# A two-layer decoder step on one core: the first query half split into prompt and sample columns, and two memory key blocks transposed, inside the norm ahead of the attention

## What is computed

```
x = post_norm(x, mixer(x), ln_g[l, 0], ln_b[l, 0])
c = memory_cross_attention(x, mem_ks[l], mem_vs[l], w_q[l], w_o[l])

def post_norm(x, h, g, b):          # per token over 1024 features
    z = DN_ALPHA * x + h
    z = (z - mean(z)) * rsqrt(var(z) + LN_EPS)
    return z * g + b

def memory_cross_attention(x, mem_k, mem_v, w_q, w_o):
    q = (x @ w_q).reshape(B, T, 4, 256)
    s = einsum('bthd,bmhd->bhtm', q, mem_k) * 256 ** -0.5
    p = softmax(s)
    o = einsum('bhtm,bmhd->bthd', p, mem_v).reshape(B, T, 1024)
    return o @ w_o
```

## Time and profile before

| | |
|---|---|
| median of 3 runs | 1392.79 us (1392.18 to 1393.89) |
| the profiled execution, its own time | 1392.58 us |
| its span, first to last instruction | 1390.8 us |
| matmul engine busy | 1341.8 us (96%) |
| vector engine busy | 1019.4 us (73%) |
| scalar engine busy | 756.2 us (54%) |
| granted matmul clock, mean | 0.996 |

### The profile page before, as it was taken

One profiled execution on the slowest core, in us unless ns is written; L12 is line 12 of the kernel. 1 busy time (PEld: TensorE's weight loads), 2 busy tenths in 40 slices (PEclk: granted clock), 3 DMA queues, 4 the chain that ended last, 5 costly groups with the idle time before them and its releaser, 6 DMA issues.

```text
span 1390.8 us, 19714 instructions
## 1 busy us (share of the span) xinstructions
PE 1341.8 (96%) x7671; PEld 1114.8 (80%) x7671; DVE 1019.4 (73%) x1100; ACT 756.2 (54%) x775; POOL 149.5 (11%) x211
## 2 busy tenths in 40 slices
PE   8999999999898999999999999999899999999996
PEld 6798997788676888888887798779777788888884
DVE  4546757763578988898887356782658989898986
ACT  4444623423425876767676353332534777677765
POOL 5200246210000000000000014220000000000000
PEclk9999999999999999999999999999999999999998
DMA  9784454437964999999994455444983799999981
GB/s 284 246 269 151 150 170 138 134 124 262 371 232 155 362 360 338 352 349 348 342 359 141 134 188 178 133 161 175 372 320 131 283 368 336 356 343 342 358 319 38
DMA packets 102002, 353.67 MB, mean 254 GB/s; under 512 B 6368, under 2 KB 32496, under 8 KB 72224
## 3 DMA queue, kind: packets, MB, share of 16 engines
q1 hardware_dynamic: 97056, 336.09, 67.4%
q0 software_dynamic: 4864, 16.45, 3.5%
HBM read 332.85 MB, written 19.67 MB: 253 GB/s over the span
## 4 chain that ended last, share of the span: by engine, by line
PE 81%; DVE 8%; ACT 4%; DMA 3%; POOL 2%; issue 2%; SPq 0%; DVEq 0%; ACTq 0%; POOLq 0%
PE ps L1895 65%; DMA att_kt<-in_cache_mem_v 2%; PE ps L2263 1%; PE ps L2473 1%; PE ps L2286 1%; DVE mix_s L1604 1%; PE ps L2274 1%; PE ps L1904 1%; PE ps L1903 1%; PE ps L2005 1%; DVE x L1324 1%; DVE x L1321 1%; PE ps L2095 1%; PE ps L2416 1%; PE ps L2417 1%
## 5 line engine op out<-in xcount | busy, mean ns | idle before, releaser
L1895 PE MATMUL ps<-w_hi,xt_hi 128*128 128x512 f32 x576 | 229.6, 399 | 5.9 <-DVE w_lo L1261 2.2
L1257 DVE TENSOR_TENSOR w_lo<-raw,w_hi 128x2048 fp32r<-128x2048 f32 x62 | 141.5, 2294 | 125.4 <-ACT w_hi L837 125.4
L1895 PE MATMUL ps<-w_hi,xt_lo 128*128 128x512 f32 x576 | 225.5, 391 | 0.0
L1895 PE MATMUL ps<-w_lo,xt_hi 128*128 128x512 f32 x512 | 200.4, 391 | 0.0
L837 ACT ACTIVATE w_hi<-raw 128x2048 fp32r<-128x2048 f32 x64 | 121.7, 1913 | 143.7 <-PE ps L1895 58.0
L1261 DVE TENSOR_TENSOR moe_lo<-moe_in_raw,w_hi 128x2048 fp32r<-128x2048 f32 x72 | 164.2, 2290 | 22.6 <-ACT w_hi L844 22.6
L1261 DVE TENSOR_TENSOR w_lo<-raw,w_hi 128x2048 fp32r<-128x2048 f32 x72 | 164.8, 2291 | 16.6 <-ACT w_hi L844 16.2
L844 ACT ACTIVATE w_hi<-moe_in_raw 128x2048 fp32r<-128x2048 f32 x72 | 138.1, 1918 | 56.4 <-PE ps L1895 56.4
L844 ACT ACTIVATE w_hi<-raw 128x2048 fp32r<-128x2048 f32 x72 | 137.5, 1912 | 14.8 <-PE ps L1895 14.8
L1895 PE MATMUL ps<-xt_hi,w_hi 128*128 128x320 f32 x448 | 138.6, 309 | 0.2
L1895 PE MATMUL ps<-xt_hi,w_lo 128*128 128x320 f32 x448 | 138.4, 309 | 0.0
(11 more groups left out here) (408 smaller groups left out, 2574.0 us busy)
## 6 DMA issues: line engine op xcount, KB each, us to landing
raw<-in_moe_w_gate SPq DMA_DIRECT2D x48, 1024.0 KB, 5.0
moe_in_raw<-in_moe_w_down SPq DMA_DIRECT2D x48, 1024.0 KB, 4.9
moe_in_raw<-in_moe_w_up SPq DMA_DIRECT2D x32, 1024.0 KB, 5.6
raw<-in_moe_w_up SPq DMA_DIRECT2D x32, 1024.0 KB, 5.6
raw<-in_hgrn_w_in SPq DMA_DIRECT2D x16, 1024.0 KB, 5.5
raw<-in_cache_mem_k SPq DMA_DIRECT2D x16, 1024.0 KB, 6.0
moe_in_raw<-in_moe_w_gate SPq DMA_DIRECT2D x16, 1024.0 KB, 5.8
raw<-in_moe_w_down SPq DMA_DIRECT2D x16, 1024.0 KB, 4.9
```

The lines of the kernel that those rows point to most:

```text
L1257: nc.vector.tensor_tensor(lo_at(slot_of(k)), raw_at(slot_of(k)), hi_at(hi_slot(k)).bitcast(F32), ALU.subtract).then_inc(w_low, 1)
L1895: ins = mm(out, lhs, rhs, start=start and n == 0, stop=stop and n == 2, skip_group_check=shared)
```

## The change

- SP loads key blocks 0 and 1 (`EARLY = 2`) into the probability tile `att_p`, once the memset has marked it as free, behind the first query chunk and ahead of the second. The later stream of loads has seven key blocks.
- The matmul engine transposes the eight quarters of these blocks inside `block_norm`: two behind tile 0's transposes, three behind tile 1's, three more behind a first part of the queries. The fillers of this norm go (those of the other norm stay).
- The first query half is cut in three: rows 0 to 255 for the 256 prompt columns behind tile 1's transposes, rows 256 to 511 for the prompt columns behind tile 2's, and all four groups of rows for the 64 sample columns once tile 2 is split.
- The vector engine splits tile 1 between the sample tile's addition and its statistics, in place of behind its norm.
- The scalar engine makes all eight copies of the early quarters, and the high part of the second query chunk, inside the norm.
- POOL makes the low part of the second query chunk too.
- The attention begins with key block 2, then the prompt's scores, then blocks 3 to 5.

```
+EARLY = 2
+KEYS = BATCHES - EARLY
+KV_CHUNKS = KEYS + 2
+EARLY_BANKS = (4, 7, 5, 4, 7, 5, 4, 6)
...
         # SP
-                dense(done, last, groups)
+                dense(done, done + 1, groups)
+                sp.wait_ge(at_z, l + 1)
+                for n in range(EARLY):
+                    sp.dma_start(early_keys(n).rearrange("p (t u c) -> p t u c", t=2, u=2), memory(l, "k", n)).then_inc(first_in[n], 16)
+                dense(done + 1, last, groups)
...
         # POOL
-                split_query(chunk_no(first_block(l) + IN_BLOCKS[l] + 2), groups)
+                for half in range(2):
+                    split_query(chunk_no(first_block(l) + IN_BLOCKS[l] + 2) + half, groups)
...
         # ACT, layer_norm; q % 3 == 0 is the norm behind the mixer
+                def keys_early(pieces):
+                    for i in pieces:
+                        n, s = i // 4, i % 4
+                        act.wait_ge(at_tr, 4 * BATCHES * (q // 3) + i + 1)
+                        nc.scalar.activation(st_att["kt"][:, n, 2 * s:2 * s + 2, :], ps[:, EARLY_BANKS[i], :].rearrange("p (b m) -> p b m", b=2),
+                                             ACT.Copy).then_inc(at_kv if s % 2 else at_ka, 1)
...
+                if q % 3 == 0:
+                    keys_early(range(0, 2))
...
+                if q % 3 == 0:
+                    turned(u, 1)
+                    split(splits[0], groups)
+                    splits[0] += 1
+                    keys_early(range(2, 3))
                 tile_rstd(q, 2)
+                if q % 3 == 0:
+                    keys_early(range(3, 8))
...
         # DVE, block_norm, between tile 2's addition and its statistics
                         ins.then_inc(evac[par], 1)
+                        if q % 3 == 0:
+                            turned(u, 1)
...
         # PE
+            def query_products(db, groups, kts, first, last):
+                k = chunk_no(db)
+                pe.wait_ge(w_low, at(k + 1, groups, GCH))
+                for kt in kts:
+                    for n in range(4):
+                        cols = slice(n * P, (n + 1) * P)
+                        ins = three(ps[:, 4 * (db % 2) + n, first:last], w_hi[:, hi_slot(k), kt, cols], w_lo[:, slot_of(k), kt, cols],
+                                    xt_hi[:, kt, first:last], xt_lo[:, kt, first:last], kt == 0 and first == 0, False, True, True)
...
+            def keys_turned(l, pieces):
+                for i in pieces:
+                    n, s = i // 4, i % 4
+                    if s == 0:
+                        pe.wait_ge(first_in[n], 16 * (l + 2))
+                    if i in (3, 5):
+                        pe.wait_ge(at_ka, 2 * BATCHES * l + i // 2)
+                    elif i in (4, 6):
+                        pe.wait_ge(at_kv, 2 * BATCHES * l + i // 2 - 1)
...
                 turn(q, u, 0)
+                if q % 3 == 0:
+                    keys_turned(q // 3, range(0, 2))
                 tile_block(db, groups, 2)
                 turn(q, u, 1)
-                keep_busy(18 if q % 3 == 0 else 20, 7)
-                turn(q, u, 2)
+                if q % 3 == 0:
+                    keys_turned(q // 3, range(2, 5))
+                    pe.wait_ge(xt_l, turns(u, 1) + 2)
+                    query_products(db + 1, groups, range(0, 2), 0, PROMPT)
+                    keys_turned(q // 3, range(5, 8))
+                    pe.wait_ge(at_ka, 2 * BATCHES * (q // 3) + 3)
+                    turn(q, u, 2)
+                    query_products(db + 1, groups, range(2, 4), 0, PROMPT)
+                    pe.wait_ge(xt_l, turns(u, 2) + 1)
+                    query_products(db + 1, groups, range(0, 4), PROMPT, NT).then_inc(w_used, 1)
...
-                dense(db + 2, groups, "T")
+                dense(db + 2, groups, "T", halves=(1,))
                 dense(db + 3, groups, "T")
...
-                keys_in(0)
-                keys_in(1)
+                keys_in(2)
                 prompt_scores()
-                for n in range(2, 6):
+                for n in range(3, 6):
```

More of the change, by code:

```diff
@@ L833, in split @@
                 elif 0 <= k - keys_no(0 if k < CHUNKS0 else 1) - KV_CHUNKS < NH:
-                    act.wait_ge(w_used, at(keys_no(0 if k < CHUNKS0 else 1) + BATCHES + 2, groups, GCH))
+                    act.wait_ge(w_used, at(keys_no(0 if k < CHUNKS0 else 1) + KV_CHUNKS, groups, GCH))
                 elif k >= NH:
@@ L895, in turned, with layer_norm @@
                                          ps[:, turn_bank0(u, t) + half, :].rearrange("p (k s) -> p k s", s=n), ACT.Copy).then_inc(xt_h, 1)
-            def layer_norm(q, u, moe=False):
+            def layer_norm(q, u, moe=False, groups=None):
                 def rows_hi(t):
@@ L1072, in _ @@
                 split_ahead(db + 1, groups, 3)
-                layer_norm(3 * l, 2 + 3 * l)
+                layer_norm(3 * l, 2 + 3 * l, groups=groups)
                 act.wait_ge(at_z, l + 1)
@@ L1927, in memory_chunk, with dense @@
                     ins.then_inc(w_used, 1)
-            def dense(db, groups, mode, tiles=TILES):
+            def dense(db, groups, mode, tiles=TILES, halves=(0, 1)):
                 par = db % 2
@@ L1933, in dense @@
                     pe.wait_ge(evac[par], db // 2)
-                for half in range(2):
+                for half in halves:
                     k = chunk_no(db) + half
@@ L1953, in dense @@
                                 ins = three(ps[:, 4 * par + n, 0:NT], w_hi[:, rh, kc, cols], w_lo[:, r, kc, cols],
-                                            xt_hi[:, kt, 0:NT], xt_lo[:, kt, 0:NT], start, stop, True)
+                                            xt_hi[:, kt, 0:NT], xt_lo[:, kt, 0:NT], start, stop, True, len(halves) == 1)
                         else:
@@ L2015, in turn @@
                         ins.then_inc(xt_ps, 1)
-                if t == 2:
+                if t == 2 and q % 3:
                     keep_busy(5, 5 if q % 3 < 2 else 4)
                     pe.wait_ge(xt_l, turns(u, t) + 1)
+            def keys_turned(l, pieces):
+                for i in pieces:
+                    n, s = i // 4, i % 4
+                    rows = early_keys(n).rearrange("p (t c) -> p t c", t=2)
+                    if s == 0:
[4 more added lines that the diff above has]
+                        pe.wait_ge(at_kv, 2 * BATCHES * l + i // 2 - 1)
+                    for b2 in range(2):
+                        for mh in range(2):
+                            ins = nc.tensor.transpose(ps[:, EARLY_BANKS[i], b2 * MEM + mh * P:b2 * MEM + (mh + 1) * P],
+                                                      rows[:, mh, (2 * s + b2) * P:(2 * s + b2 + 1) * P], ident[:])
+                    ins.then_inc(at_tr, 1)
             def block_norm(db, groups, q, u):
@@ L2024, in block_norm @@
                 turn(q, u, 0)
+                if q % 3 == 0:
+                    keys_turned(q // 3, range(0, 2))
                 tile_block(db, groups, 2)
                 turn(q, u, 1)
-                keep_busy(18 if q % 3 == 0 else 20, 7)
-                turn(q, u, 2)
+                if q % 3 == 0:
[8 more added lines that the diff above has]
+                    query_products(db + 1, groups, range(0, 4), PROMPT, NT).then_inc(w_used, 1)
+                else:
+                    keep_busy(20, 7)
+                    turn(q, u, 2)
             def transpose_in(u, src, tiles, kts):
```

32 lines of the change are left out of this document (16 added, 16 removed).

## The result

The changed kernel takes **1402.25 us** (median of 4 runs, 1400.40 to 1406.61) against 1392.49 us (1391.50 to 1393.89) for the kernel before in the same job: a ratio of 1.0074 with a 95% interval of 1.0049 to 1.0099. It is slower by 9.8 us. I had forecast 1387.2 us with a range of 1382.0 to 1391.6 and a chance of 0.10 for slower. The profiled execution of the changed kernel is its slowest, 1406.61 us with a span of 1404.9 us, and its mean granted clock is 0.986; the other three have 0.988 to 0.990, and the kernel before has 0.996.

The account below looks back on a forecast made before the run. The matmul engine, 96% busy, was taken as the bound, with gains only where it lacks useful work. +1.8 and -4.5 make -2.7 us a layer, -5.4 for two: 1392.58 - 5.4 = 1387.2 us, range 1382.0 to 1391.6.

Parts of the forecast that it names:

- POOL makes the second low part: In layer 0's second norm: POOL's 4.61 us, from 293.9 to 298.5, wanted only at 306.3, would cost nothing.
- my -2.7 us a layer: Net forecast per layer: +1.8 us before the query ends and -4.5 us after it.
- the forecast T: End of the four query halves in layer 0: 325.88 us before the change, forecast near 327.6.
- The clock rival: Clock falls behind the norm's stall and transposes, slowing prompt matmuls: +5.0 to +11.4 us a layer, 1397 to 1410; chance 0.09.
- The stall ahead of the prompt part: Matmul engine's wait for tile 1's splitting in the norm, before the first 24 prompt matmuls: 0.45 us.
- Prompt scores: In the attention, they start 1.95 us after the query halves end, with one block's key transposes remaining ahead.
- the last load: Last value block of the attention lands 45.7 us after the query halves end, before the change 50.2.
- my -4.5: Attention saving per layer, as two key blocks leave the saturated load stream: -4.5 us, ends -2.5 and -5.5.
- The rivals on the load stream: Last value block lands only 2.5 us sooner, so a layer saves 0.7 us: 1391.2 us; chance 0.15.
- the price of the sample columns: 64-column matmuls at 0.08 us gain 1.6 us more a layer: 1384.0, chance 0.07; at 0.148 us, 1390.4.
- The forecast of +1.8 us for the division: In the norm, the first query half's sample columns end at 306.3 against 304.55: +1.8 us, 0.2 to 3.4.

Follow-up runs that it names:

- e6: The changed kernel with one wait on POOL, so its second low part starts only after the vector engine's norm of the third tile: 1390.69 us.
- e4: The kernel before, with only the second query chunk's high part earlier on the scalar engine and its low part on POOL: 1401.71 us.
- e1: The changed kernel with the second query chunk's low part back on the vector engine, behind its norm: 1391.08 us.
- e5: The changed kernel with the second low part back on the vector engine and 3 fillers between each of the four groups of 64-column matmuls: 1390.88 us.
- e3: The changed kernel reduced to the early keys: first query half undivided, second low part on the vector engine, 10 fillers added: 1382.81 us.
- e7: The kernel with the early keys alone, without its 10 fillers, so the matmul engine idles before the third tile's transposes: 1386.65 us.
- e2: The changed kernel with 15 fillers in the wait ahead of tile 2's transposes, the low part left on POOL: 1399.03 us.

## Why the prediction was wrong

**The step that failed** is "POOL makes the second low part, 4.61 us from 293.9 to 298.5; wanted at 306.3, cost nothing". Its length and place are right (4.58 us from 294.06). I asked only who waits for the result and not what else runs meanwhile. It ran beside a scaling of the vector engine with two operands in SBUF (`x` and `ln_gb`), and that scaling stood still until POOL was done: 5.48 us in place of 1.28. e6 and e4 show it from both sides, by taking the overlap out of the changed kernel (11.6 us less) and by putting it into the kernel before (1401.71 us).

A second term stood at nothing in the sum: **the clock**. Of the 15.1 us between the forecast and the median, the overlap explains about 11.6 by e6, with the wait and the fall of the clock behind it. The remaining 3.5 us fit the fall at the 64-column matmuls, which e6 and e1 keep and e5 removes: it costs 5.2 us over both layers of e1's profile, while the division and the attention came out a little cheaper than in my sum.

The Trainium skill (SBUF — State Buffer, "SBUF: two separate sides") states it: the two engines share one pair of ports, which is "an exclusive lock, not a bandwidth split", and an operation of the vector engine with two SBUF inputs needs it against one of POOL that reads SBUF. All rows here agree: 5.48 and 4.42 us with the overlap, 1.27 without it. In the earlier trace rows the first low part, on POOL from 276.00 to 280.6, gave no warning: beside it the vector engine ran additions with one operand in PSUM (276.49, 0.69 us) and statistics (277.21), at full speed. But the trace of the kernel before held the warning elsewhere, the other way round. Two equal copies on POOL, and what the vector engine did beside the second:

```profile
35.35 0.18 POOL L661 COPY own_rows<-ident 32x8 f32<-32x8 f32 x1
...
35.84 2.17 POOL L661 COPY own_rows<-ident 32x8 f32<-32x8 f32 x1
```
```profile
35.66 2.29 DVE L1257 TENSOR_TENSOR w_lo<-raw,w_hi 128x2048 fp32r<-128x2048 f32 x1 [0.42 <-ACT w_hi L837]
```

The low part reads two operands in SBUF and started first; the small copy ended 0.06 us behind it.

By this rule of the Trainium skill the scaling, which my schedule started at 294.1, would have waited for POOL's end at 298.5, and the norm would have ended at 298.5 + 2 x 1.28 = 301.1 in place of 296.7. That is 3.6 us past the 297.45 at which it is wanted, and turns my -2.7 us a layer into +0.9, before any fall of the clock.

**From the forecast T to the measured one.** The blocked scaling adds 5.48 - 1.27 = 4.2 us. The third tile's transposes, which I had at 297.45, start at 301.17, 3.7 us later, since 0.75 us of it was covered and the rest of the norm is some tenths late. From there to T the changed kernel takes 36.07 us, and e5's lengths at the full clock (8 transposes in 0.64 us, then 29.29 us) make 29.93: 6.1 us for the clock, of which 3.4 stand in e1 too and 2.7 come behind the wait. Together 9.9 us; 327.6 became 337.24, 9.6 us. Twice 9.86 us on the forecast of 1387.2 makes 1406.9, and the profiled execution took 1406.61. That it comes out so close is partly luck: in layer 1 the profile has 1.6 us more ahead of the norm, in the mixer, and 0.7 us less in the attention, which this sum leaves out. The median is 4.4 us lower, with a higher clock in its runs.

**The clock rival** had 0.09, and I let it start behind 20 transposes. It doesn't: e3 runs 12 key transposes right ahead of the query half at a clock of 1.00. What I had not asked is what the clock would do behind a wait on the path (e7) and in the 64-column matmuls (e1, e5). I had priced a half-clock 256-column matmul at 0.105 us more; measured 0.21 against 0.12 us, 0.09 more. For the 64-column ones I had reckoned no price, as I took their columns to be what the clock touches. They went from 0.112 to 0.213 us too: at either level they cost nearly as much as 256 columns do.

**What held.**
- 256 columns: forecast 0.120 us, measured 0.12. 64 columns with full weights: forecast 0.115, measured 0.112 at the full clock. The whole query end at full clock would have been 329.40 - 2.34 = 327.06 us by e5, against 327.6; e5's norm runs 0.3 us ahead of that of the kernel before, so 327.35 is the fairer number.
- The stall ahead of the prompt part: 0.64 us for 0.45, the query's start 293.35 for "near 293".
- Prompt scores 1.75 us behind T for 1.95, sample scores at T + 15.0 for 15.3, the last load at T + 45.6 for 45.7. The early keys came in time, and the wait on SP cost nothing. The saving in the attention of layer 0 is 4.6 us (T + 50.3 to T + 45.7), my -4.5; in layer 1 it is 5.3.
- The rivals on the load stream and on the price of the sample columns didn't happen.

**The forecast of +1.8 us for the division** was weighed against where the first half ended before, and not against the keys alone. (It should have read +2.0: the schedule gives tile 2's transposes 0.45 us, and the row says 0.64.) Counted from the third tile's first addition, T comes after 35.66 us before, after 35.70 in e3, and after 37.13 in the divided kernel at full clock (e5 less its fillers): +1.5. The division doesn't pay but costs: where 48 matmuls of 320 columns took 7.1 us, 48 of 256 and 48 of 64 take 11.1, which is 4.0 us more, and only 24 of them, 2.9 us, go ahead of the third tile's transposes. They bring the clock's fall with them besides, 3.4 and 1.8 us in e1. In the same job e1, which is e3 with the division and without its fillers, takes 8.3 us more (1391.08 and 1382.81). All the gain of the change is in the early keys, and e3, at 10.0 us under the kernel before, has more of it than I had forecast for the whole.

**Left open:** what makes the clock fall sooner or later, or not at all. In the changed kernel it falls behind 30 and 29 of the 64-column matmuls; in e1, e2 and e6 behind 35, 38 and 41 in one layer and only behind all 48 in the other. Which trait of these matmuls does it, and why the fillers of e5 prevent it, no run separates. Each kernel's profile is one execution, so differences of 1 to 2 us between stretches of two kernels are not explained here. One such: in layer 1's mixer the matmul engine waits 2.1 us for a low part. Behind that wait the clock of the changed kernel was 0.50 from 915 to 918 us, and it fell there in e1, e2, e4, e5 and e7 too; in the kernel before, e3 and e6 it stayed at 1.00.

## What to carry to other kernels

When a step is moved to an engine that has time, ask for each of its microseconds which operation of the vector engine runs beside it, and how many operands that one reads from SBUF; one wait that keeps POOL clear of a norm on the path was worth 11.6 us. Split a matmul group only if the narrow part is cheaper than its share: with full weights 64 columns cost 0.112 us and 320 cost 0.148. And test the parts of a change alone: here the early keys were worth 10.0 us (e3), the division without fillers cost 8.3 (e1 against e3) and the move to POOL 11.2 (the changed kernel against e1), which add up to the 9.8 us of the whole but for 0.3 us between the jobs.

## What the runs showed of the hardware that I had not expected

- The granted clock goes to the 1.2 GHz level in the middle of matmuls without a gap: in e1, behind 35 matmuls with 64 columns and full weights, at 100% busy. With 3 fillers of 512 columns between the groups of 12 (e5) it stays at 1.00 from 300 to 330 us, and in layer 1 from 938 to 980.
- At that level matmuls of 64 and of 256 columns both come every 0.213 us; at the full clock every 0.112 and 0.120 us.
- A vector operation held by POOL is shown as busy for the whole time (5.48 us), with no wait in the profile, and so is a POOL operation held by the vector engine (2.17 us in place of 0.18). Only the length beside that of its twin tells it.
